# Hybrid encoder layer, one core: the final norm's work shared between ScalarE, GpSimd and VectorE

## What is computed

```python
h = h + 0.5 * g2[:, None, :] * _swiglu(_modulate(h, sh2, s2), ffn2_wg[i], ffn2_wu[i], ffn2_wd[i])
h = _rms(h) * g_final[i]        # h * rsqrt(mean(h*h) + 1e-6) * g_final
```

## Time and profile before

| | |
|---|---|
| median of 3 runs | 1918.24 us (1916.04 to 2536.94) |
| profiled execution | 1917.56 us, span 1915.8 us |
| TensorE busy | 1839.4 us, 96% of the span |
| VectorE busy | 1386.7 us, 72% |
| ScalarE busy | 797.1 us, 42% |
| GpSimd busy | 804.0 us, 42% |

### The profile page before, as it was taken

One profiled execution on the slowest core, in us unless ns is written; L12 is line 12 of the kernel. 1 busy time (PEld: TensorE's weight loads), 2 busy tenths in 40 slices (PEclk: granted clock), 3 DMA queues, 4 the chain that ended last, 5 costly groups with the idle time before them and its releaser, 6 DMA issues.

```text
span 1915.8 us, 22675 instructions
## 1 busy us (share of the span) xinstructions
PE 1839.4 (96%) x8039; PEld 1469.5 (77%) x8039; DVE 1386.7 (72%) x1774; ACT 797.1 (42%) x1252; POOL 804.0 (42%) x605
## 2 busy tenths in 40 slices
PE   4999999999999999997999999999999999999997
PEld 3788888788888878985655656877888888888886
DVE  6678888886777785776888876358656555577778
ACT  4532232233344554237676643154332333334443
POOL 1076655665200010019999952014566556520000
PEclk9999999999999999997999999999999999999999
DMA  9046666545753442000000024112233323476333
GB/s 352 17 138 195 213 217 194 195 162 199 251 209 94 121 175 64 9 1 0 1 1 0 0 66 154 67 55 94 99 111 109 110 83 110 171 252 226 99 106 125
DMA packets 132795, 232.11 MB, mean 121 GB/s; under 512 B 8780, under 2 KB 66227, under 8 KB 132434
## 3 DMA queue, kind: packets, MB, share of 16 engines
q1 hardware_dynamic: 132500, 230.73, 35.6%
q10 hardware_dynamic: 190, 0.01, 0.0%
HBM read 177.75 MB, written 52.95 MB: 120 GB/s over the span
## 4 chain that ended last, share of the span: by engine, by line
PE 36%; POOL 7%; issue 6%; DVE 5%; DMA 1%; ACT 1%; POOLq 0%; ACTq 0%; DVEq 0%
PE ps L502 19%; PE ps L854 9%; PE ps L2756 5%; POOL cv L1816 3%; PE ps L1657 1%; POOL cv L1815 1%; PE ps L376 1%; PE ps L1635 1%; DVE T L935 1%; POOL slot L1766 0%; POOL rqk L1751 0%; DMA wor<-in_w_out 0%; POOL wor L1910 0%; POOL slot L1762 0%; DVE ring L479 0%
## 5 line engine op out<-in xcount | busy, mean ns | idle before, releaser
L502 PE MATMUL ps<-T,ring 128*128 128x512 f32 x1920 | 441.9, 389 | 0.0
L502 PEld LDWEIGHTS ps<-T,ring 128*128 128x128 f32 x1920 | 360.4, 188 | 75.2 <-DVE ring L479 0.2
L502 PE MATMUL ps<-B,ring 128*128 128x512 f32 x1440 | 340.0, 393 | 4.5 <-DVE SG L561 2.5
L502 PEld LDWEIGHTS ps<-B,ring 128*128 128x128 f32 x1440 | 271.2, 189 | 63.7 <-issue 7.6
L954 POOL TENSOR_SCALAR stat<-stat 128x1 f32<-128x1 f32 x32 | 10.6, 332 | 548.4 <-ACT XS L879 258.9
L568 POOL TENSOR_TENSOR HID<-HID,SG 128x512 f32<-128x512 f32 x80 | 122.0, 1525 | 263.2 <-DVE HID L553 152.3
L854 PE MATMUL ps<-PW 128*128 128x512 f32 x924 | 217.2, 389 | 0.0
L854 PE MATMUL ps<-PT 128*128 128x512 f32 x900 | 212.0, 390 | 0.0
L854 PEld LDWEIGHTS ps<-PW 128*128 128x128 f32 x924 | 173.3, 188 | 36.0
L479 DVE TENSOR_TENSOR ring<-sums,ring 128x512 fp32r<-128x512 f32 x160 | 162.9, 1027 | 52.3 <-ACT ring L473 52.3
L854 PEld LDWEIGHTS ps<-PT 128*128 128x128 f32 x900 | 168.5, 188 | 34.8
(11 more groups left out here) (337 smaller groups left out, 3305.1 us busy)
## 6 DMA issues: line engine op xcount, KB each, us to landing
adat<-ffn_hidden SPq DMA_DIRECT2D x154, 256.0 KB, 2.6
ada_raw<-in_w_ada SPq DMA_DIRECT2D x56, 512.0 KB, 4.1
rawg<-in_ffn_wg SPq DMA_DIRECT2D x22, 1024.0 KB, 5.5
rawu<-in_ffn_wu SPq DMA_DIRECT2D x22, 1024.0 KB, 5.2
ffn_hidden<-HID SPq DMA_DIRECT2D x84, 256.0 KB, 2.7
ffn_hidden<-base SPq DMA_DIRECT2D x66, 256.0 KB, 2.6
H<-in_x SPq DMA_DIRECT2D x16, 512.0 KB, 6.5
h_saved_rows<-H SPq DMA_DIRECT2D x16, 512.0 KB, 2.6
```

The costliest lines, as they stand in the source:

```text
L502: mm = e.matmul(ps[:, product_bank(M, k)], ring[:, place % RING, wx, kc], RIGHT[k][:, xx, kc], start=(kc == 0 and i == 0), stop=(kc == HC ...
```

## The change

ScalarE multiplies each of the first four rows by its factor inside the last product, after the cuts of steps 67 to 70 (`first_scale`). GpSimd then multiplies each by g_final, and those rows are stored from there. VectorE no longer has finals 0 to 3.

At the end, tile 7's right half (C22, complete earlier) is squared and summed on ScalarE, and its mean plus epsilon made on GpSimd, ahead of the rest; VectorE multiplies that half by g_final. Of tile 7's left half, the part of C21 that does not depend on P4 (V) is weighted and added to `H` ahead; when P4's tile is there, it is weighted straight out of PSUM and added. ScalarE squares the left half only; the last mean adds both. ScalarE scales the right half, VectorE scales and multiplies the left half, and each half is stored by itself.

```diff
-        def pool_rstd(e, base):
-            for t in range(NT):
+        def pool_rstd(e, base, tiles=range(NT)):
+            for t in tiles:
...
-            for t in range(NT):
-                e.wait_ge(o_ok, t + 1)
+            for t in range(THALF):
+                e.wait_ge(tail_pool, t + 1)
                 e.dma_start(out_d[:, t], H[:, t]).then_inc(final_out, 16)
-            e.wait_ge(final_out, 16 * NT)
+            for t in range(THALF, LAST_TILE):
+                e.wait_ge(tail_dve, ROW_OUT[t])
+                e.dma_start(out_d[:, t], H[:, t]).then_inc(final_out, 16)
+            e.wait_ge(tail_act, TAIL_HALF)
+            e.dma_start(out_d[:, LAST_TILE, HALF:D], H[:, LAST_TILE, HALF:D]).then_inc(final_out, 16)
+            e.wait_ge(tail_dve, ROW_OUT[LAST_TILE])
+            e.dma_start(out_d[:, LAST_TILE, 0:HALF], H[:, LAST_TILE, 0:HALF]).then_inc(final_out, 16)
+            e.wait_ge(final_out, 16 * (NT + 1))
...
-            pool_rstd(e, FINAL)
+            pool_rstd(e, FINAL, range(THALF))
+            e.wait_ge(gfin_in, 16)
+            for t in range(THALF):
+                e.wait_ge(tail_act, t + 1)
+                e.tensor_tensor(H[:, t], H[:, t], gfin, ALU.mult).then_inc(tail_pool, 1)
+            e.wait_ge(tail_act, TAIL_SQUARE)
+            e.tensor_scalar(stat[:, TAIL_MEAN], stat[:, TAIL_SUM], 1.0 / D, EPS, ALU.mult, ALU.add).then_inc(tail_pool, 1)
+            pool_rstd(e, FINAL, range(THALF, LAST_TILE))
+            e.wait_ge(sumsq, FINAL + NT)
+            e.wait_ge(tail_pool, TAIL_MEAN_OK)
+            e.tensor_scalar(stat[:, NT + LAST_TILE:2 * NT], stat[:, LAST_TILE:NT], 1.0 / D, stat[:, TAIL_MEAN], ALU.mult, ALU.add)\
+                .then_inc(mean_sq, 1)
+            e.wait_ge(mean_sq, FINAL + NT)
+            e.tensor_tensor(stat[:, 2 * NT + LAST_TILE:3 * NT], stat[:, NT + LAST_TILE:2 * NT], mhalf[:, LAST_TILE:NT], ALU.pow)\
+                .then_inc(rms_inv, 1)
...
+            def first_scale(t):
+                e.wait_ge(rms_inv, FINAL + t + 1)
+                e.activation(H[:, t], H[:, t], ACT.Copy, scale=stat[:, 2 * NT + t:2 * NT + t + 1]).then_inc(tail_act, 1)
+
             def final_starts(j, g):
+                if j == J_P4 and 1 <= g <= THALF:
+                    first_scale(g - 1)
...
-            for t in range(THALF, NT):
-                final_square(t)
+            e.wait_ge(tail_dve, TAIL_READY)
+            e.wait_ge(sumsq, FINAL + THALF)
+            e.activation(XS[:, THALF + 1, HALF:D], H[:, LAST_TILE, HALF:D], ACT.Square, accum_out=stat[:, TAIL_SUM]).then_inc(tail_act, 1)
+            final_square(THALF)
...
+            final_square(THALF + 1)
+            final_square(THALF + 2)
...
+            e.activation(XS[:, THALF + 1, 0:HALF], H[:, LAST_TILE, 0:HALF], ACT.Square, accum_out=stat[:, LAST_TILE:NT]).then_inc(sumsq, 1)
+            e.wait_ge(tail_dve, TAIL_GAINED)
+            e.wait_ge(rms_inv, FINAL + NT)
+            e.activation(H[:, LAST_TILE, HALF:D], H[:, LAST_TILE, HALF:D], ACT.Copy, scale=stat[:, 2 * NT + LAST_TILE:3 * NT])\
+                .then_inc(tail_act, 1)
...
-            for t in range(THALF):
-                final(t)
-            for t in range(THALF):
+            tail = H[:, LAST_TILE, 0:HALF]
+
+            def tail_ahead():
+                t = THALF - 1
+                e.wait_ge(*f.p_out(p_made("V", t)))
+                e.tensor_tensor(ub(t), ub(t), grow[:, 0:HALF], ALU.mult).then_inc(tail_dve, 1)
+                e.wait_ge(tail_act, TAIL_SQUARE)
+                e.tensor_tensor(H[:, LAST_TILE, HALF:D], H[:, LAST_TILE, HALF:D], gfin[:, HALF:D], ALU.mult).then_inc(tail_dve, 1)
+                e.wait_ge(tail_dve, TAIL_SCALED)
+                e.tensor_tensor(tail, tail, ub(t), ALU.add).then_inc(tail_dve, 1)
+
+            def tail_rest():
+                t = THALF - 1
+                wait_product(e, f, J_P4, t)
+                e.wait_ge(tail_dve, TAIL_AHEAD)
+                e.tensor_tensor(ub(t), bank_of(J_P4, t), grow[:, 0:HALF], ALU.mult).then_inc(tail_dve, 1)
+                e.wait_ge(tail_dve, TAIL_LAST)
+                e.tensor_tensor(tail, tail, ub(t), ALU.add).then_inc(f.added.sem, 1)
+
+            for t in range(THALF - 1):
                 for what in ("C21", "C21*", "C21+"):
                     dve_result(e, f, what, t)
-                if t >= 1:
+                if t == 0:
+                    tail_ahead()
+                else:
                     final(THALF + t - 1)
-            final(NT - 1)
+            tail_rest()
+            final(LAST_TILE - 1)
+            e.wait_ge(rms_inv, FINAL + NT)
+            e.scalar_tensor_tensor(out=tail, in0=tail, scalar=stat[:, 2 * NT + LAST_TILE:3 * NT], in1=gfin[:, 0:HALF],
+                                   op0=ALU.mult, op1=ALU.mult).then_inc(tail_dve, 1)
```

More of the change, by code:

```diff
@@ L298, in build @@
         gfin = XS[:, THALF + 2]
+        LAST_TILE = NT - 1
+        TAIL_SUM, TAIL_MEAN = slice(3 * NT + 1, 3 * NT + 2), slice(3 * NT + 2, 3 * NT + 3)
         fs = [ffn_sems(0), ffn_sems(1)]
@@ L325, in build @@
         mix_hi, mix_lo, mix_mm, mix_added = sem("mix_hi"), sem("mix_lo"), sem("mix_mm"), sem("mix_added")
-        gfin_in, o_ok = sem("gfin_in"), sem("o_ok")
+        gfin_in, tail_dve, tail_act, tail_pool = sem("gfin_in"), sem("tail_dve"), sem("tail_act"), sem("tail_pool")
+        FIRST_ROWS, TAIL_SQUARE, TAIL_HALF = THALF, THALF + 1, THALF + 2
+        TAIL_MEAN_OK = THALF + 1
+        TAIL_READY, TAIL_SCALED, TAIL_GAINED, TAIL_AHEAD, TAIL_LAST = 1, 2, 3, 4, 7
+        ROW_OUT = {THALF: 5, THALF + 1: 6, THALF + 2: 8, THALF + 3: 9}
         def sp_load_gu(e, f, w, g):
@@ L787, in dve_result @@
                         ins.then_inc(f.added.sem, 1)
+                    elif f is fs[1] and what == "C22+" and tile == LAST_TILE:
+                        ins.then_inc(tail_dve, 1)
                     return
@@ L2330, in _ @@
             act_down(e, f, final_starts)
-            for t in range(THALF, NT):
-                final_square(t)
+            e.wait_ge(tail_dve, TAIL_READY)
[5 more added lines that the diff above has]
+            final_square(THALF + 2)
+            e.wait_ge(*f.added(NT))
+            e.wait_ge(sumsq, FINAL + NT - 2)
+            e.activation(XS[:, THALF + 1, 0:HALF], H[:, LAST_TILE, 0:HALF], ACT.Square, accum_out=stat[:, LAST_TILE:NT]).then_inc(sumsq, 1)
[3 more added lines that the diff above has]
+                .then_inc(tail_act, 1)
         @block.vector
@@ L2602, in final @@
                 e.scalar_tensor_tensor(out=H[:, t], in0=H[:, t], scalar=stat[:, 2 * NT + t:2 * NT + t + 1], in1=gfin,
-                                       op0=ALU.mult, op1=ALU.mult).then_inc(o_ok, 1)
+                                       op0=ALU.mult, op1=ALU.mult).then_inc(tail_dve, 1)
             dve_down(e, f, lambda j, g: None)
             e.wait_ge(gfin_in, 16)
-            for t in range(THALF):
-                final(t)
-            for t in range(THALF):
+            tail = H[:, LAST_TILE, 0:HALF]
[3 more added lines that the diff above has]
+                e.tensor_tensor(ub(t), ub(t), grow[:, 0:HALF], ALU.mult).then_inc(tail_dve, 1)
+                e.wait_ge(tail_act, TAIL_SQUARE)
+                e.tensor_tensor(H[:, LAST_TILE, HALF:D], H[:, LAST_TILE, HALF:D], gfin[:, HALF:D], ALU.mult).then_inc(tail_dve, 1)
[9 more added lines that the diff above has]
+            for t in range(THALF - 1):
                 for what in ("C21", "C21*", "C21+"):
                     dve_result(e, f, what, t)
-                if t >= 1:
+                if t == 0:
+                    tail_ahead()
+                else:
                     final(THALF + t - 1)
-            final(NT - 1)
+            tail_rest()
+            final(LAST_TILE - 1)
+            e.wait_ge(rms_inv, FINAL + NT)
+            e.scalar_tensor_tensor(out=tail, in0=tail, scalar=stat[:, 2 * NT + LAST_TILE:3 * NT], in1=gfin[:, 0:HALF],
+                                   op0=ALU.mult, op1=ALU.mult).then_inc(tail_dve, 1)
         @block.tensor
```

## The result

The changed kernel takes 1922.52 us (median of 22 runs), the kernel before 1918.34 in as many; the ratio is 1.0023, with a 95% interval of 1.0016 to 1.003. The ratio leaves out two slow runs of the kernel before, of 2336 and 2537 us. By the ratio the change makes the kernel 4.4 us slower, 3.1 to 5.8 (the medians differ by 4.2). That is clear of the scatter of these runs, and small: 0.2% of the time. The profiled execution has 1920.66 us and a span of 1918.6.

What follows compares the result with a forecast made beforehand. The prediction took the end to be bound by a chain passing from TensorE to a late VectorE. Span 1915.8 plus 1.6 (cut delay less shorter end) plus 0.8 (clock) gave 1918.2, so 1920.6 us by the median, range 1914.5 to 1923.8.

Steps and rivals of the forecast that it cites:

- slower was its likeliest sign: Whole kernel: the likeliest case, chance 0.52, was the lock as walked through, +2.4 us on the median.
- The lock and the turns: Cuts 68 and 69: VectorE waits for whole GpSimd multiplies at the shared SBUF ports; last PX cut 6.1 us late.
- The rival in which VectorE wins that turn: Cut 68's second half goes before GpSimd's second multiply: delay 4.05 us, 1918.6 us in all; chance 0.2.
- TensorE's margin: Before the tail: TensorE's slack over the cuts is used up, steps 70 and 71 each 0.8 to 1.9 us behind.
- The clock: First tile of the tail: granted clock likely falls to 1.2 GHz for 3.4 us, costing 0.8 us, at most 1.7.
- the rival of two low stretches: Clock stays low for two stretches of 3.4 us, into tiles 1 and 2: 3.4 us lost, 1923.2 us; chance 0.15.
- The end: From the end of TensorE's last tile to the end of the span: 6.65 us in place of 11.16.
- final 6 "costs nothing": Final 6 (1.2 us) runs on VectorE while tile 7's square is made, so it adds nothing unless tile 6's factor is late.
- The gain that was to pay for it: With TensorE's end unmoved, span 1911.3 us, 4.5 less: 2.56 from VectorE's lateness, the rest from the shorter end.
- VectorE does not wait for products in the last tiles: Last tiles: the prediction claimed VectorE would wait for products, needing 3.3 us a tile against TensorE's 3.40.
- The sum: Whole kernel: span 1915.8 + 1.6 + 0.8 = 1918.2 us, so +2.4 on the median, 1920.6 us.
- they take turns: Shared SBUF ports: GpSimd and VectorE instructions with two SBUF inputs alternate, each holding the ports for a whole instruction.

Runs made afterwards that it cites:

- e7: Changed kernel with one wait more: GpSimd's second multiply starts only when both halves of cut 68 are done; ratio to the kernel before 1.0003.
- e1: Changed kernel without ScalarE's scalings and GpSimd's multiplies inside the last product, new end kept; ratio to the kernel before 0.9999.
- e4: Changed kernel with multiplies of rows 0 to 2 placed in VectorE's gaps and beside its PSUM readers, row 3 left to VectorE; ratio to the kernel before 0.9978.
- e5: Changed kernel with ScalarE's scalings kept, the four multiplies made by VectorE after its last cut instead of GpSimd; ratio to the kernel before 1.0011.
- e6: Changed kernel with all four GpSimd multiplies waiting for the last cut of the last product; ratio to the kernel before 1.0008.
- e8: The kernel e4 with tile 7 stored by one DMA of 512 KB in place of two of 256 KB; ratio to the kernel before 0.9988.
- e3: Changed kernel with each of GpSimd's four multiplies cut in two of half a row, same work; ratio to the kernel before 0.9997.
- e2: Kernel before with only the scalings on ScalarE and the multiplies on GpSimd added, old end kept; ratio to the kernel before 1.0023.

## Why the prediction was right

The forecast of 1920.6 us, in a range of 1914.5 to 1923.8, holds the measured 1922.52, and slower was its likeliest sign. Its steps, each against the profile of the changed kernel:

- **The lock and the turns.** The last cut was to be 6.1 us late, and is 6.34 late. The order at 1873, where the margin was 0.1 us, went as walked: GpSimd's second multiply started at 1872.32, 0.22 us before cut 68's second half asked. That this turn fell so was close, and 1.9 us hung on it. The rival in which VectorE wins that turn is what e7 makes; its delay was put at 4.05 us and is 4.41.
- **TensorE's margin.** It is used up by step 69, and steps 70 and 71 wait 0.58 us each. The last matmul was to move by what the last cut moves, plus the clock: 6.34 and 0.96 make the 7.30 us measured.
- **The clock.** It fell, was low for 3.4 us, and was to cost 0.8. From the last cut to the last matmul it takes 11.2 us in before, e1, e4, e5, e6 and e8, 12.19 in the changed kernel (31.42 - 20.19 against 38.72 - 26.53): 0.96 us. In e3 it fell in the stretch 1895 to 1896, so that it lay over tile 5, and cost 12.84 - 11.23 = 1.61 us; in e7 1.2. The bound of 1.7 holds in all. In e7 the clock was low for 6.8 us, from 1895.9 to 1902.7, which is the length that the rival of two low stretches has; but the last cut ends only at 1900.23, up to there TensorE went at the pace of the cuts, and it cost 1.2 us, not the rival's 3.4. In all four kernels in which the clock fell (changed, e2, e3 and e7) the price is near half of the low time that lies behind the last cut. So the length of a low stretch does not give its price; what matmuls lie under it does. In none of them did the clock fall a second time before the last matmul, as the Trainium skill (TensorE: Matmul & The Clock Gate, HAM oscillation) would let one fear.
- **The end.** From the last matmul to the end of the span 6.65 us were forecast and 7.32 measured. That is the term that was mis-sized. GpSimd, VectorE, ScalarE and SyncE's queue in the changed kernel:

```profile
1904.38 0.59 POOL L962 TENSOR_SCALAR stat<-stat 128x1 f32<-128x1 f32 x1 [5.23 <-ACT XS L2348]
...
1913.61 0.46 POOL L2141 TENSOR_SCALAR stat<-stat 128x1 f32<-128x1 f32 x1 [1.30 <-ACT XS L2375]
1914.15 0.55 POOL L2144 TENSOR_TENSOR stat<-stat,mhalf 128x1 f32<-128x1 f32 x1
```

```profile
1904.23 0.68 DVE L2663 TENSOR_TENSOR H<-H,xt 128x512 f32<-128x512 f32 x1
...
1912.66 1.28 DVE L2649 SCALAR_TENSOR_TENSOR H<-H,stat,XS 128x1024 f32<-128x1024 f32 x1
```

```profile
1914.80 0.72 ACT L2378 ACTIVATE H<-H,stat 128x512 f32<-128x512 f32 x1 [1.29 <-POOL stat L2144]
```

```profile
1915.92 0.43 SPq L2067 DMA_DIRECT2D out<-H  x1
```

GpSimd's last mean (L2141) takes 0.46 us, not 0.19; ScalarE's scaling takes 0.72, not the 0.63 of a plain copy; and a store of 256 KB needs 2.68 us to the end of the span, not 2.4. These three make 0.27 + 0.09 + 0.28 = 0.64 of the 0.67 us. The 0.27 points at a step of the prediction: final 6 "costs nothing" while the square is made. The mean starts inside VectorE's final 6, which has two inputs in SBUF, and ends 0.13 us after it (1913.94); in all eight kernels with the new end it ends 0.13 or 0.14 us after final 6. GpSimd's plain mean (L962) takes 0.19 us in the changed kernel where VectorE is idle or reads PSUM, and 0.59 at 1904.38, where it starts inside such an instruction and ends 0.06 us after it. So the lock, which the prediction counted against VectorE alone, worked against GpSimd here. How much of the 0.27 us the second operand of this mean takes is not separated: it never ran outside final 6.
- **The gain that was to pay for it.** That the span gets 4.5 us shorter if P3, the end of TensorE's last tile, stays is what e4 tests: it gains 42.58 - 39.09 = 3.49 us with TensorE's end moved by only 0.22. With the 0.22 and the 0.67 of the end and what VectorE is late by (it takes up the last tile at 1904.30, 0.25 us after the product, where 0.1 was assumed), 4.5 becomes 3.5. VectorE does not wait for products in the last tiles, as the prediction had it: in the changed kernel it starts on tiles 5, 6 and 7 at 1904.83, 1908.08 and 1911.33 without a gap, 3.25 us a tile against TensorE's 3.40, and catches up 0.15 us with each. And e1 shows that the gain needs both parts: with VectorE late, the shorter end alone gives 0.1 us.
- **The sum.** Counted from the start of the last product, +2.4 us were forecast and +3.46 measured; of the 1.06 us missed, 0.24 are the lock, 0.16 the clock and 0.67 the end. The times say +4.4, with 3.1 to 5.8; the forecast's +2.4 lies below that interval, so the sign and the mechanism were right and the size was small by a quarter to more than a half.

## What to carry to other kernels

Before elementwise work is given to an idle GpSimd, look at what VectorE does beside it. If that is an instruction with two SBUF inputs on the path that ends last, a GpSimd instruction can cost it nearly its whole length (here 2.2 us of 2.4). Short instructions halved the delay here (2.97 us in place of 6.34), one added wait took 1.9 us off it, and with three rows placed in VectorE's gaps and beside its PSUM readers, and the fourth left to VectorE, 0.22 us was left. A shorter end pays only once the engine that takes up the last result is no longer late on it.

## What was not expected

- In e1 and e5 the last store landed about 0.9 us later than in the other kernels with two stores: 3.6 us from the second issue to the end of the span (1914.41 to 1918.0 in e1), where the changed kernel, e3, e4, e6 and e7 have 2.6 to 2.7. In e1's last stretches the DMA share falls to 0.07 and 0.01 over a whole microsecond before the end, in place of stopping:

```profile
1916.50:1917.00 0.50, 0.00 (x0) 0.00 (x0) 0.00 (x0) 0.00 (x0) 0.00 (x0) 0.50 0.07 20
1917.00:1917.50 0.50, 0.00 (x0) 0.00 (x0) 0.00 (x0) 0.00 (x0) 0.00 (x0) 0.50 0.01 4
```

  It looks as if a few late packets held up the whole store. That, and what makes them late, stays open; no run was made for it.
- The start of the last product moves by up to 3.8 us between profiles of kernels that are the same up to there. A comparison of two single spans would have put e1 2.2 us above before, with nothing in it but 0.85 at the end.
- In e5 GpSimd did not get its turn. Its first mean for tile 7 starts inside the second of the four PX cuts and ends at 1900.04, 0.05 us after VectorE's four multiplies (1899.99), so it waited while six further instructions with two SBUF inputs ran on VectorE. GpSimd's timeline in e5, and then VectorE's:

```profile
1893.95 6.09 POOL L2135 TENSOR_SCALAR stat<-stat 128x1 f32<-128x1 f32 x1 [23.55 <-ACT XS L2366]
```

```profile
1892.95 2.50 DVE L715 TENSOR_TENSOR PX<-adat,PX 128x512 fp32r<-128x512 f32 x4
1895.36 4.63 DVE L2654 TENSOR_TENSOR H<-H,XS 128x1024 f32<-128x1024 f32 x4
```

  It cost nothing there, as nothing waited for that mean. But "they take turns", as the prediction has it, is what the cuts and the multiplies do, and not a rule for every pair of instructions. What decides it stays open.
